# Two more up-projection slots of each layer in the seven-product form, with the work that prepares them redistributed

## The reference, cut to what matters

```python
def conv_gated_mlp(h, w_up, conv_w, conv_b, w_down):
    s = h.shape[1]
    up = h @ w_up                                     # 1024 -> 2 * 2816
    half = CONV_W // 2
    pad = jnp.pad(up, ((0, 0), (half, half), (0, 0)))
    conv = sum(pad[:, j:j + s] * conv_w[j] for j in range(CONV_W)) + conv_b
    a, b = jnp.split(conv, 2, axis=-1)
    return (jax.nn.gelu(a) * b) @ w_down

x = x + conv_gated_mlp(rmsnorm(x, g_ffn[l]), w_up[l], conv_w[l], conv_b[l], w_down[l])
```

## Time and profile before

| | |
|---|---|
| median of three runs | 1683.22 us |
| the profiled execution | 1683.37 us |
| its span | 1681.6 us |
| TensorE busy | 1673.0 us, 99% |
| VectorE busy | 1004.9 us, 60% |
| ScalarE busy | 832.6 us, 50% |
| GpSimd busy | 805.6 us, 48% |

### The profile page before, as it was taken

The page is one execution under the profiler, slowest core; times in us unless marked ns, Lnnn a source line. Parts: engine busy times, 40 slices in busy tenths (PEclk is TensorE's granted clock), DMA queues, the critical chain, the costliest instruction groups (busy, mean ns, idle before and its releaser), DMA issues.

```text
span 1681.6 us, 24045 instructions
## 1 busy us (share of the span) xinstructions
PE 1673.0 (99%) x8873; PEld 1445.6 (86%) x8873; DVE 1004.9 (60%) x1640; ACT 832.6 (50%) x1509; POOL 805.6 (48%) x808
## 2 busy tenths in 40 slices
PE   9999999999999999999999999999999999999998
PEld 7888888888888899988888888888888888999886
DVE  4778876533338967661246788755333489666642
ACT  4676754222245566662255667432223555667322
POOL 3444332433354788854344334334333547888432
PEclk9999999999999999999999999999999999999999
DMA  7422223233333333342352222322342423333422
GB/s 253 136 76 76 76 97 105 75 100 112 129 135 100 101 101 101 102 162 94 97 197 82 94 76 76 101 97 78 100 150 85 142 98 101 101 101 101 163 95 82
DMA packets 147319, 182.77 MB, mean 109 GB/s; under 512 B 3040, under 2 KB 130706, under 8 KB 146194
## 3 DMA queue, kind: packets, MB, share of 16 engines
q1 hardware_dynamic: 147090, 181.35, 32.6%
q10 hardware_dynamic: 128, 0.09, 0.0%
HBM read 170.92 MB, written 10.50 MB: 108 GB/s over the span
## 4 chain that ended last, share of the span: by engine, by line
PE 98%; ACT 0%; DVE 0%; POOL 0%; issue 0%; ACTq 0%; POOLq 0%
PE banks L1852 19%; PE banks L1853 19%; PE banks L1854 19%; PE banks L2088 6%; PE banks L2093 5%; PE banks L2089 5%; PE banks L1887 3%; PE banks L1888 3%; PE banks L1889 3%; PE banks L2167 2%; PE banks L2169 2%; PE banks L2168 2%; PE banks L1916 2%; PE banks L1943 2%; PE banks L2018 1%; PE banks L1927 1%
## 5 line engine op out<-in xcount | busy, mean ns | idle before, releaser
L630 POOL TENSOR_TENSOR w_lo<-raw,w_hi 128x256 fp32r<-128x256 f32 x636 | 514.2, 843 | 784.9 <-ACT w_hi L732 784.9
L1852 PE MATMUL banks<-xg_hi,w_hi 128*128 128x512 f32 x896 | 350.2, 391 | 0.0
L1853 PE MATMUL banks<-xg_lo,w_hi 128*128 128x512 f32 x896 | 349.1, 390 | 0.0
L1854 PE MATMUL banks<-xg_hi,w_lo 128*128 128x512 f32 x896 | 348.7, 389 | 0.0
L1279 DVE TENSOR_TENSOR w_lo<-raw,w_hi 128x768 fp32r<-128x768 f32 (+2 forms) x118 | 100.9, 855 | 175.0 <-ACT w_hi L731 174.8
L1854 PEld LDWEIGHTS banks<-xg_hi,w_lo 128*128 128x128 f32 x896 | 168.2, 188 | 35.5
L1852 PEld LDWEIGHTS banks<-xg_hi,w_hi 128*128 128x128 f32 x896 | 168.4, 188 | 33.8 <-issue 0.2
L1853 PEld LDWEIGHTS banks<-xg_lo,w_hi 128*128 128x128 f32 x896 | 168.4, 188 | 33.5 <-issue 0.2
L731 ACT ACTIVATE w_hi<-raw 128x768 fp32r<-128x768 f32 (+2 forms) x119 | 87.4, 735 | 173.4 <-PE banks L1854 87.9
L732 ACT ACTIVATE w_hi<-raw 128x1280 fp32r<-128x1280 f32 (+3 forms) x119 | 158.8, 1335 | 0.0
L673 POOL TENSOR_TENSOR a_lo<-raw,a_hi 128x1024 fp32r<-128x1024 f32 (+1 forms) x56 | 104.9, 1874 | 40.2 <-ACT a_hi L1042 40.2
(11 more groups left out here) (239 smaller groups left out, 3845.2 us busy)
## 6 DMA issues: line engine op xcount, KB each, us to landing
raw<-in_w_in SPq DMA_DIRECT2D x55, 1024.0 KB, 5.1
raw<-in_w_up SPq DMA_DIRECT2D x44, 1024.0 KB, 5.1
raw<-in_w_br SPq DMA_DIRECT2D x16, 1024.0 KB, 5.0
raw<-in_w_down SPq DMA_DIRECT2D x12, 1024.0 KB, 5.1
x_spill<-x_res SPq DMA_DIRECT2D x4, 2048.0 KB, 7.4
x_res<-x_spill SPq DMA_DIRECT2D x4, 2048.0 KB, 9.5
raw<-in_w_out SPq DMA_DIRECT2D x8, 1024.0 KB, 5.1
raw<-in_w_down SPq DMA_DIRECT2D x8, 896.0 KB, 4.7
```

The source lines that it names most:

```text
L630: last = nc.gpsimd.tensor_tensor(w_lo[p_][:, k, :], raw[p_][:, k, :], f32(w_hi[p_][:, k, :]), ALU.subtract)
L1852: nc.tensor.matmul(out, w_hi[w][:, k, cols], x_hi[:, a, :], start=first and k == 0, stop=False)
L1853: nc.tensor.matmul(out, w_hi[w][:, k, cols], x_lo[:, a, :], start=False, stop=False)
L1854: mm = nc.tensor.matmul(out, w_lo[w][:, k, cols], x_hi[:, a, :], start=False, stop=last and k == kt - 1)
```

## The change

NS goes from 8 to 6, so two plain slots of each layer become blocks (16 in place of 14). The work that prepares the token side is put at other half slots. On VectorE the eight normalisations go from halves (1,0) to (2,1), two each, to halves (0,0), (0,1) and (1,0), four, two and two; the sums stand one each at (1,1), (2,0), (2,1) and (3,0); the low halves stand at (2,1), (3,1) twice, and (4,0). ScalarE rounds the seven operands at (1,0) to (3,0), and rounds the weights of slot n + 2 ahead of the centre tap of half (n, 1), where this stood behind it. GpSimd makes operand 5 first, right behind the split of slot 2, and operands 4 and 6 behind the split of slot 4; its wait for the four sums ahead of operand 5 goes.

```diff
-NS = 8
+NS = 6
...
-    H_VECTOR, H_POOL = (0, 1, 2, 3), (4, 5, 6)
+    H_VECTOR, H_POOL = (0, 1, 2, 3), (5, 4, 6)
...
                 if q == 5:
                     pool.wait_ge(spilled2, 16 * l + 16)
-                    pool.wait_ge(h_t_ok, l * 4 + 4)
...
             for s in range(S_F + 2, S_S):
                 split(s)
-                if s >= S_S - 3:
-                    operand_lo(H_POOL[s - S_S + 3])
+                for q in {S_F + 2: (5,), S_F + 4: (4, 6)}.get(s, ()):
+                    operand_lo(q)
...
-            hi_at = {(3, 0): H_ACT[0:3], (3, 1): H_ACT[3:5], (4, 0): H_ACT[5:7]}
+            hi_at = {(1, 0): H_ACT[0:1], (1, 1): H_ACT[1:3], (2, 0): H_ACT[3:4], (2, 1): H_ACT[4:6], (3, 0): H_ACT[6:7]}
...
+                    if half and 0 < n < NS - 2:
+                        split(S_F + n + 2)
                     conv_centre(n, half)
                     if (n, half) == (NS - 2, 1):
                         for b in range(4):
                             block_hi(0, b)
-                    if half and 0 < n < NS - 2:
-                        split(S_F + n + 2)
...
-            sums_at = {(2, 1): (0,), (3, 0): (1, 2), (3, 1): (3,)} if NS == 6 else {(3, 0): (0, 1), (3, 1): (2, 3)}
-            lows_at = {(3, 1): (0,), (4, 0): (1, 2), (4, 1): (3,)} if NS == 6 else {(4, 0): (0,), (4, 1): (1,), (5, 0): (2,), (5, 1): (3,)}
+            norms_at = {(0, 0): (0, 1, 2, 3), (0, 1): (4, 5), (1, 0): (6, 7)}
+            sums_at = {(1, 1): (0,), (2, 0): (1,), (2, 1): (2,), (3, 0): (3,)}
+            lows_at = {(2, 1): (0,), (3, 1): (1, 2), (4, 0): (3,)}
...
-                    if 1 <= n <= 2:
-                        for m in range(4 * n + 2 * half - 4, 4 * n + 2 * half - 2):
-                            normalise(m)
+                    for m in norms_at.get((n, half), ()):
+                        normalise(m)
```

## The result

The changed kernel takes 1685.59 us, the median of 20 runs (1684.94 to 1689.22), beside 1683.03 us for 20 runs of the kernel before (1682.31 to 1686.60): a ratio of 1.0015, 95% interval 1.0008 to 1.0022. That is 2.6 us more, small and real, and 0.2 us above the forecast. The profiled execution took 1685.78 us, its span 1684.0.

The account below looks back on a forecast made before the run. TensorE's stream was taken as the bound, with VectorE short among its feeders: 1683.4 - 3.0 + 2 x (0.4 + 2.2) = 1685.6 us, median 1685.4; 8-in-10 range 1681.0 to 1687.8.

Parts of the forecast that it names:

- The floor: TensorE, four plain slots becoming blocks at 10.13 instead of 10.88 us: 3.0 us less, 1680.4 from the profiled 1683.4.
- VectorE 44.5 of 44.9 us: VectorE before the blocks: 44.5 us of work must go into 44.9; before, it had 10.7 us to spare.
- Rounding ahead of the centre tap: ScalarE: centre tap at most 1.9 us later, hidden at no cost; bound 0.6 us of VectorE idle in half (2,1).
- Crossings as an exclusive lock: VectorE instructions with two SBUF operands and GpSimd ones never overlap; with shared bandwidth instead, no wait and 1680.4 us.
- The walk: Stepping all four queues: each instruction starts when its engine is free and its last wait has ended, using lengths from the profile.
- TensorE waits 0.4 us at slot 3 and 2.2 at the third product: Waits per layer for GpSimd's split (bounds 0 to 1.6) and ScalarE's seed in block 0 (bounds 0 to 2.9).
- rival C: Waits at slot 3 feed VectorE time: 1.6 there leaves 1.3 at the seed; 1685.2 to 1686.8; forecast included, chance 0.6.
- The sum, 2.6 a layer: TensorE's waits of 0.4 and 2.2 us, in two layers: 1683.4 - 3.0 + 2 x 2.6 = 1685.6, median 1685.4.
- Nothing waits after block 0: VectorE catches up, as a block leaves it 30% idle, so nothing waits up to block 5.
- What would show it: Profile signs: 192 fewer plain matmuls, 10.13 us blocks, split and seed as releasers, VectorE without idle from about 517.
- Rival A: No new TensorE wait anywhere: 1680.4 us (median 1680.3); chance 0.13.
- Rival B: VectorE's split for slot 5 late by up to 1.6 us: 4.2 us of waits a layer, 1688.8 us; chance 0.1.

Follow-up runs that it names:

- Experiment 4: Changed kernel with sums 0 and 1 on GpSimd, operand 5 behind slot 3's split, and block 0's third-product seed ahead of the last centre tap: 1680.48 us.
- experiment 3: Changed kernel with ScalarE's weight rounding put back behind the centre tap: 1690.76 us.
- experiment 1: Changed kernel with eight plain slots again (NS = 8), all else as changed: 1684.31 us.
- experiment 5: Changed kernel with ScalarE's seed of block 0's second bank ahead of the last plain half's centre tap, nothing else: 1684.86 us.
- experiment 7: Changed kernel with ScalarE rounding operand 5 ahead of operand 3: 1685.91 us.
- experiment 2: Changed kernel with GpSimd's low half of operand 5 behind slot 3's split instead of ahead of it: 1687.83 us.
- experiment 6: Changed kernel with sums 0 and 1 on GpSimd and operand 5 behind slot 3's split, seed left behind the last centre tap: 1680.70 us.

## Why the prediction was right, point by point

- *The floor, 3.0 us from four slots.* Right. Experiment 4, without these waits, has a median of 1680.48 where 1680.3 was worked out.
- *VectorE 44.5 of 44.9 us.* The size is right: until evacuation (4,1) it was busy 45.10 us. With what it waited for ScalarE's taps and TensorE this took 47.54.
- *Normalising in the wait for the first tap.* Right: four pieces in 2.71 us, and 0.81 of the 3.43 us of idleness is left.
- *Rounding ahead of the centre tap, at no cost.* Right for the total, and more: without it the waits are 5.2 us a layer (experiment 3). But the tap of half (2,1) doesn't hide: VectorE stands 0.81 us for it, above the bound of 0.6.
- *Weight loads at nothing.* Right: ScalarE's staging copy of block 2 waits 1.62 us for its load (its row at 570.80), three times the bound, but it comes after both waits of layer 0, and TensorE has no later one there.
- *Crossings as an exclusive lock.* The walk had the start of evacuation (5,1) at 563.3; it came at 563.03 in a trace whose first evacuation is 0.26 us earlier than before, so 563.29. Halves (3,1) and (4,1), walked at 539.9 and 551.5, came at 540.0 and 551.6 on the same footing. With bandwidth shared, the prediction's walk had 1680.4. The Trainium skill, SBUF — State Buffer, "SBUF: two separate sides", has VectorE with two SBUF inputs and GpSimd exclude each other for a whole instruction. The trace agrees: sum 2 takes 1.21 us with a split of 6.29 in the changed kernel, and 1.81 with one of 5.22 in experiment 1, so one of the two waits out the other.
- *TensorE waits 0.4 us at slot 3 and 2.2 at the third product.* Here the division is wrong, 1.63 and 1.05. The step that failed is the crossing of sum 2 with the last piece of slot 3's split. The walk had the split's end at 529.4; it came at 530.25, with sum 2 ahead of that piece. The prediction's words don't fit its number: it has sum 2 between the pieces at a wait of 0.4, and no wait with sum 2 behind the last one. The traces show 1.63 with sum 2 ahead of the last piece alone, and 0.55 with it behind (experiments 1 and 5), where the split takes 5.2 us, about what the walk gave it (524.1 to 529.4). The bound of 1.6 and rival C, with 1.6 and 1.3, had the other outcome. The two instructions start within 0.01 us of each other, and the walk can't tell 0.01 us. Experiment 1's expectation, which took the outcome of the changed kernel for a property of the order, missed for the same reason.
- *The sum, 2.6 a layer.* Right, 2.68 and 2.62. That a wait at slot 3 shortens the one at the entry is shown: the number didn't hang much on who wins the crossing, since the other outcome gave 2.3 in experiment 5. That it agrees to 0.1 us is luck: for the crossing as it fell, the prediction's own reckoning was 2.9.
- *Nothing waits after block 0.* Wrong by 0.28 us in block 3 of layer 1, a sign that the prediction had named against itself. ScalarE's copy into m comes at 1428.55, 0.54 us after TensorE starts the third product; in layer 0 it was 0.26. The seed that follows on ScalarE ends at 1431.08, and TensorE starts the fifth product at 1431.13. Why that copy comes later is open.
- *What would show it.* The counts, the period of 10.13 us and the split as releaser came true. Of the rest, the page gives "issue" and not the seed as releaser of the second wait; VectorE does have idle time behind 517; and evacuation (5,1) comes 1.99 us behind block 0's first matmul, not 3, because the wait at slot 3 had already moved that matmul.

In the profiled execution: 1683.37 - 3.0 + 2.68 + 2.62 + 0.28 = 1685.95 us, against 1685.78. What the sum lacks lies ahead of the change: the first rms-scaled evacuation comes 0.26 us earlier than in the execution of before. It comes up to 1.04 us earlier in other experiments (503.05 in 5 and 7), and with this difference, and the slow stretches counted in, the same sum gives each profiled time to 0.15 us. So the 0.28 us that were not foreseen and the earlier start nearly cancel in the forecast's favour.

Rival A, no wait, was right about what is possible and wrong about this order. Rival B's wait before slot 5 came up as soon as operand 5 was moved (experiment 2), at 3.4 us a layer and not at 4.2.

## What to carry to other kernels

When TensorE is full, shortening its stream shortens the time in which the others prepare, so add up the busiest feeder's work, its collisions included, against the room that is left, before counting the gain. A wait that is removed without giving time to the late engine comes back at its next deadline (experiments 5 and 7); ask of each wait who is late, and move work off that engine into a neighbour's idle time (here two sums to GpSimd, with the order that goes with them, 1685.6 to 1680.7 us). Where two instructions that exclude each other are due within some hundredths of a microsecond, forecast both outcomes and trust only what is the same in either.

## What the runs showed of the hardware that was not expected

- After waits of alike length the granted clock fell in one layer and not in the other. It was 0.54 behind an idle time of 1.88 us in layer 0 of experiment 7 and 1.00 behind 1.90 us in layer 1; 0.50 behind 3.12 us in layer 1 of experiment 3 and 1.00 behind 3.18 us in layer 0. The low level cost 1.5 us in experiment 7, where TensorE has no later wait that it could shorten, and next to nothing in experiment 3, where the loss gave VectorE time. The clocks of the runs tell how often this happens. In experiment 7 five lie at 1685.2 to 1685.4 us, all with a mean granted clock of 0.999, and six at 1685.9 to 1686.6, all with 0.998; the slow stretch of the profiled one, 3.6 us at 0.54, is worth 0.001 of the mean. Of the changed kernel's 20, only the one at 1686.95 us has 0.998. In experiment 2 five lie at 1686.5 to 1687.2 with 0.999 or 1.000, and five from 1688.5 up, three of them with 0.997 or 0.998; in the other two something else must add to it. What makes the clock fall behind one wait and not behind its like isn't known.
- Some executions of several of these kernels, that of before among them, are about 3.5 us longer (3 of its 20 beside the changed kernel). Two of the profiled ones, of experiments 1 (1687.72 us) and 6 (1684.25 us), were such, and in both the time is lost at the start of the program, far ahead of the change. Here is a stretch of experiment 1, in the same columns as the stretches above:

```profile
7.00:13.50 6.50, 6.50 (x17) 4.03 (x16) 2.69 (x4) 0.83 (x2) 1.87 (x1) 1.00 0.67 216
```

The same stretch of the changed kernel:

```profile
7.00:13.50 6.50, 6.50 (x31) 4.70 (x30) 4.72 (x8) 3.69 (x7) 3.02 (x2) 1.00 0.86 288
```

TensorE starts 17 matmuls there in place of 31, and eight 512-column ones took 3.78 us together in place of 2.27. They start 0.427 us apart, the spacing of the slow stretch in experiment 3, though the row here gives the granted clock as 1.00. VectorE's first rms-scaled evacuation then comes at 507.27 instead of 503.83. What decides between the two was not tried.
